# A two-block transformer on one core: block order of the down projection, one expert tile between top-k and gates, and where the first early expert group is made

## What is computed

```python
def first_block(...):
    h = h + hybrid_mixer(rmsnorm(h), ...)
    h = h + cross_attention(rmsnorm(h), rmsnorm(mem), ...)
    h = h + conv_ffn(rmsnorm(h), w_up, ffn_dw_w, w_down)
    return rmsnorm(h, norm_final_g)

def conv_ffn(h, w_up, ffn_dw_w, w_down):
    up = causal_dwconv(einsum("bsd,df->bsf", h, w_up), ffn_dw_w)
    z = silu(up[..., :D_FF]) * up[..., D_FF:]          # D_FF = 2816 = 22 blocks of 128
    return einsum("bsf,fd->bsd", z, w_down)

def second_block(...):
    ...                                                 # stick-breaking attention, gated delta rule, merge
    x = x + peer_ffn(rms_norm(x), w_q, keys1, keys2, u_tab, v_tab)

def peer_ffn(h, ...):                                   # 8 heads, 128 x 128 = 16384 experts, 16 per head
    s1, s2 = scores of the two halves of the query against 128 keys each
    v1, i1 = top_k(s1, 16); v2, i2 = top_k(s2, 16)
    vals, c = top_k(all sums v1 + v2, 16)
    expert, gate = from (i1, i2, c), softmax(vals)
    act = gelu(h @ u_tab[expert])                       # one column of u per chosen expert
    return sum over chosen experts of gate * act * v_tab[expert]
```

## Time and profile before

| what | us |
|---|---|
| median of 3 runs | 3472.61 (3469.71 to 3473.6) |
| the profiled execution's own time | 3472.78 |
| its span (first to last instruction) | 3470.6 |
| TensorE busy in it | 3325.0 (96%) |
| VectorE busy | 2271.6 (65%) |
| GpSimd busy | 1835.0 (53%) |
| ScalarE busy | 773.9 (22%) |
| DMA, mean over the span | 113 GB/s |

### The profile page before, as it was taken

One profiled execution on the slowest core, in us unless ns is written; L12 is line 12 of the kernel. 1 busy time (PEld: TensorE's weight loads), 2 busy tenths in 40 slices (PEclk: granted clock), 3 DMA queues, 4 the chain that ended last, 5 costly groups with the idle time before them and its releaser, 6 DMA issues.

```text
span 3470.6 us, 40765 instructions
## 1 busy us (share of the span) xinstructions
PE 3325.0 (96%) x15978; PEld 2735.4 (79%) x15978; DVE 2271.6 (65%) x3397; ACT 773.9 (22%) x1201; POOL 1835.0 (53%) x994
## 2 busy tenths in 40 slices
PE   7989899999999999899999999999999999999998
PEld 5777678877876787888788888888888887888887
DVE  7975279953316255776563888799964334787784
ACT  2132322211126222222211111145531111111110
POOL 4536267766442454100466666633346665676675
PEclk9999999999999999999999999999999999999999
DMA  3212122222220121000232344345553335555552
GB/s 134 73 55 97 43 90 96 96 89 89 99 71 33 61 86 66 20 13 13 85 106 98 140 138 142 137 158 204 188 203 119 118 122 182 194 191 191 190 186 98
DMA packets 164270, 391.70 MB, mean 113 GB/s; under 512 B 10736, under 2 KB 69104, under 8 KB 162032
## 3 DMA queue, kind: packets, MB, share of 16 engines
q1 hardware_dynamic: 73408, 262.70, 22.2%
q10 hardware_dynamic: 90672, 126.39, 10.7%
HBM read 326.14 MB, written 62.91 MB: 112 GB/s over the span
## 4 chain that ended last, share of the span: by engine, by line
PE 71%; DVE 24%; issue 2%; ACT 2%; POOL 0%; DMA 0%; ACTq 0%; DVEq 0%; POOLq 0%
PE banks L1381 19%; PE banks L1382 19%; PE banks L1383 19%; DVE sb_gated L1287 6%; DVE sb_sq L2026 3%; DVE sb_onehot L1284 2%; PE banks L704 1%; PE banks L367 1%; PE banks L715 1%; DVE sb_tmp L2036 1%; PE banks L712 1%; DVE banks L1903 1%; PE banks L384 1%; DVE sb_tmp L1327 1%; DVE sb_cacc L1903 1%
## 5 line engine op out<-in xcount | busy, mean ns | idle before, releaser
L1369 POOL TENSOR_TENSOR sb_wL<-sb_raw,sb_wH 128x1024 fp32r<-128x1024 f32 x495 | 1209.1, 2443 | 1604.1 <-PE banks L1383 1538.5
L1381 PE MATMUL banks<-sb_hH,sb_wH 128*128 128x512 f32 x2040 | 820.2, 402 | 9.1 <-DVE sb_hL L496 2.6
L1382 PE MATMUL banks<-sb_hL,sb_wH 128*128 128x512 f32 x2040 | 798.9, 392 | 0.0
L1383 PE MATMUL banks<-sb_hH,sb_wL 128*128 128x512 f32 x2040 | 798.8, 392 | 0.0
L1364 POOL TENSOR_SCALAR sb_wH<-sb_raw 128x1024 fp32r<-128x1024 f32 x495 | 641.9, 1297 | 14.6 <-DMA sb_raw<-in_weights 14.6
L1381 PEld LDWEIGHTS banks<-sb_hH,sb_wH 128*128 128x128 f32 x2040 | 386.4, 189 | 95.8 <-issue 14.8
L1383 PEld LDWEIGHTS banks<-sb_hH,sb_wL 128*128 128x128 f32 x2040 | 385.5, 189 | 82.2
L1382 PEld LDWEIGHTS banks<-sb_hL,sb_wH 128*128 128x128 f32 x2040 | 386.3, 189 | 77.9 <-issue 3.6
L1381 PE MATMUL banks<-sb_pzH,sb_wH 128*128 128x512 f32 x1024 | 401.7, 392 | 13.5 <-DVE sb_pzL L1331 11.3
L1382 PE MATMUL banks<-sb_pzL,sb_wH 128*128 128x512 f32 x1024 | 399.6, 390 | 0.0
L1383 PE MATMUL banks<-sb_pzH,sb_wL 128*128 128x512 f32 x1024 | 399.5, 390 | 0.0
(11 more groups left out here) (420 smaller groups left out, 4804.5 us busy)
## 6 DMA issues: line engine op xcount, KB each, us to landing
sb_raw<-in_weights SPq DMA_DIRECT2D x495, 512.0 KB, 3.2
gates<-sb_stage ACTq DMA_DIRECT2D x16, 2048.0 KB, 7.8
acts<-sb_sq ACTq DMA_DIRECT2D x96, 256.0 KB, 2.0
sb_Gt<-gates ACTq DMA_DIRECT2D x24, 1024.0 KB, 7.0
sb_Ga<-acts ACTq DMA_DIRECT2D x24, 1024.0 KB, 10.4
sb_Gt<-gates ACTq DMA_DIRECT2D x4, 2048.0 KB, 10.1
sb_xT<-in_xT SPq DMA_DIRECT2D x4, 512.0 KB, 10.2
acts<-sb_xT ACTq DMA_DIRECT2D x1, 2048.0 KB, 7.8
```

What stands on the lines that cost most here:

```text
L1369: nc.gpsimd.tensor_tensor(wL[:, t % LOS, :], raw[:, t % RAWS, :], wH[:, t % HIS, :].bitcast(F32), ALU.subtract).then_inc(sems("weights_lo" ...
L1381: pe.matmul(out, hi, H, start=start, stop=False)
L1382: pe.matmul(out, hi, L, start=False, stop=False)
L1383: return pe.matmul(out, lo, H, start=False, stop=stop)
```

## The change

1. A list `DOWN` gives the order of the 176 blocks of the down projection: rows d = 0 and d = 1 share it, first f = 0 to 15 of row 0, then f = 0 to 15 of row 1, then f = 16 to 21 of row 0 and of row 1. The other rows are as they were. The host packs the weights in the same order.
2. Between top-k and gates the meeting goes. TensorE runs one early u tile behind the last `turn_slots` and ACT its gelu; DVE waits only for the 12 copies to `sb_slots`. As the early u tiles are 96 as before, 31 of them are left for the 32 gate steps, and the last step has its four products without a tile.
3. In the last late group DVE no longer adds the 8 v tiles in a loop of its own. `early_group(-1, 0)` adds them one by one between the parts of early group 0.

```diff
+DOWN = [(_d, _f) for _f0, _f1 in ((0, 16), (16, FFB)) for _d in (0, 1) for _f in range(_f0, _f1)]
+DOWN += [(_d, _f) for _d in range(2, KB) for _f in range(FFB)]
...
             turn_slots(3)
-            E.meet()
+            one_tile(t0 + n, h_hi, h_lo)
+            n += 1
...
                 gate_products(4 * i + 1)
-                one_tile(t0 + n, h_hi, h_lo, ready=lambda k: gate_products(4 * i + k // 3 + 1) if k in (3, 6) else None)
+                if n < 8 * EARLY:
+                    one_tile(t0 + n, h_hi, h_lo, ready=lambda k: gate_products(4 * i + k // 3 + 1) if k in (3, 6) else None)
+                else:
+                    gate_products(4 * i + 2)
+                    gate_products(4 * i + 3)
...
             keep_slots(3)
-            E.meet()
+            early_gelu(n)
+            n += 1
...
-                    if r % 4 == 3:
+                    if r % 4 == 3 and n < 8 * EARLY:
                         early_gelu(n)
...
-            E.meet()
+            E.eng.wait_ge(sems("slots_copied"), 12)
             for j in range(TG):
...
-                for d in range(8):
+                for d in range(8 if g < LATE - 1 else 0):
                     t = t0 + 8 + d
                     tile_ready(E, t)
...
-                    if i is not None and e < 8:
+                    if e < 8:
                         t = t0 + 8 * i + e
                         tile_ready(E, t)
...
-                early_group(z - 1 if z else None, z if z < EARLY else None)
+                early_group(z - 1, z if z < EARLY else None)
...
-                        d, f = divmod(8 * (t - t0) + k, FFB)
+                        d, f = DOWN[8 * (t - t0) + k]
...
-    downs = down.reshape(FFB, P, 8, P).transpose(2, 0, 1, 3).reshape(22, 8, P, P).transpose(0, 2, 1, 3).reshape(22, P, D)
+    blocks = down.reshape(FFB, P, 8, P).transpose(2, 0, 1, 3)
+    downs = np.stack([blocks[d, f] for d, f in DOWN]).reshape(22, 8, P, P).transpose(0, 2, 1, 3).reshape(22, P, D)
```

## The result

The kernel after takes **3453.84 us** (median of 4 runs, 3452.01 to 3455.37), the kernel before 3472.61 beside it (4 runs, 3469.71 to 3473.6). The ratio is 0.9947 [0.9935, 0.9959]: 0.5% faster, 18.8 us. 3455.3 was predicted. The span of the profiled execution fell from 3470.6 to 3453.0, by 17.6.

The account below looks back on a forecast made before the run. TensorE was taken to set 71% of the time, with VectorE setting the gates' pace. Terms of 8.0 + 0.9 + 8.5 = 17.4 us off 3472.78 gave 3455.4, on the median 3455.2; it said 3455.3, range 3450 to 3462.

Parts of the forecast that it names:

- the time of the last z: Down projection: VectorE makes the last z at 737.65, or 740.7 with one GpSimd low part costing 3.02 us.
- rival 3: Down projection: two GpSimd parts cost 6.0 us, z comes 1.3 us late, up to 4; 3457 to 3459, chance 0.07.
- margin of 1.7 us: Down projection: the last z, at 740.7, still comes 1.7 us ahead of its block at 742.4.
- The early start: Start of the gates: TensorE's early start is used up by waiting, so the start of the rows hardly moves.
- (c): Gates: VectorE is behind from the start, so its 1.1 us of idle time go: -1.1 us.
- (a): End of the gates: the last step has no tile, only a product of about 0.9 us: -3.3 us.
- The second path: Last gates store to first late group's load to fifth late tile: store goes out at about 2569.4, 0.9 us earlier.
- The bound of +1: Tile between top-k and gates: +1 us if the 1.1 us do not come back and the store-load chain not either.
- rival 2: Early group 0: its load lands 3 us later, TensorE stops at tile 3; 3458 to 3461 us, chance 0.09.
- pays in full: Tile between the stages: GpSimd's extra part hides and both paths move by 3.9 us; 3452.3 us, chance 0.12.
- another rhythm: Gates: VectorE finds its ring full in every step, then is locked out by GpSimd; 34 us, 3489 in all, chance 0.02.
- missing large term: One of the two large terms is missing, for instance through another stop right behind; 3463.5 us, chance 0.05.

Follow-up runs that it names:

- e10: The kernel after with the first two down rows split at f = 19 instead of 16: 3452.77 us in one run.
- e9: The kernel after with the first two down rows split at f = 12 instead of 16: 3461.47 us in one run.
- e11: The kernel after with the two halves of early group 0 loaded in the other order, second half first: 3466.62 us in one run.
- second comparison: The kernel after, unchanged, measured once more against the kernel before: 3459.0 us against 3470.27, ratio 0.9958.
- e2: The kernel before with the tile between top-k and gates alone: 3473.92 us, ratio 1.001.
- e1: The kernel before with the new order of the down blocks alone: 3465.53 us, ratio 0.9983.
- e3: The kernel before with early group 0 made beside the last late v tiles alone: 3463.09 us, ratio 0.9979.

## Why the prediction came out as it did

The total is right: 3453.84 lies in 3450 to 3462, 1.5 us from 3455.3. Its working is right in two terms and wrong in one.

**Part 1 held** (-8.0 predicted, -7.6 measured). That the low clock would go with the wait held too: of the 7.6 us only 5.30 were idle. The Trainium skill (TensorE: Matmul & The Clock Gate, section "What's actually happening") has the halved clock as the idle state; by that rule more than the idle time is saved, and the runs agree (7.6 against 5.3). The step that was too generous is the time of the last z. One low part of GpSimd was reckoned on its way, there were two (behind tiles 2 and 3, at 736.82 and 742.26), as rival 3 had it. The prediction's own numbers had the second: tile 3 ends one tile, 5.44 us, behind tile 2's 733.5, so ahead of its z at 740.7. Against the start of the loop z came 25.5 us behind it, which is 742.7 in the times of before, not 740.7; the block was due at 742.4. Rival 3's mechanism was there, its price 0.4 us instead of 1.3 to 4, since the second part met only the two last low parts of z (3.48 us instead of 1.47) and TensorE went on without a longer stop. The margin of 1.7 us was in truth none; a split at 19 gives it, as e10 shows.

**Part 2 failed** (-0.9 predicted, +2.5 measured). Two steps of it held. The early start was used up by waiting: the first row comes only 0.1 us earlier. And GpSimd's work behind the extra tile costs 3.0 (306.0 - 302.9 = 3.1; the earlier trace rows gave 3.02). The Trainium skill (SBUF - State Buffer, section "SBUF: two separate sides") says that the loser of the shared port waits for a whole instruction of the other. The prediction set that against the low part's 2.43 us alone; with the high part behind it GpSimd works for 3.5 us, and the measured 3.0 to 3.1 stays below that, so the rows don't speak against the page.

Two steps failed. First (c), that VectorE's 1.1 us of idle time go because it is behind from the start: it stood idle for 1.2 us all the same. The extra part held back its second row, TensorE waited 2.82 us for that row and then ran at the low clock, and VectorE found its ring full at rows 7 and 8; in e9, with the clock at 1.00 there, the idle time is gone. Second (a), -3.3 us for the empty last step, with its product "at full clock": from the last gated to the first late tile it took 2.39 us instead of 0.9, so 1.8 were saved and not 3.3, and the late tiles behind it, the first at the low clock, lost 1.4 that the prediction put at nothing. The pieces are -0.1, +3.1, -1.8 and +1.4, together the +2.5 of the stretch within 0.1. Both failed steps are one: the prediction had priced the low clock wherever a stop went, and forgot it where one was made. The second path did not count: the store went out at 2559.82, the load at 2566.27, and the fifth late tile did not wait. (The prediction's 2569.4 for that store is 0.2 above its own terms, 2567.2 + 0.9 + 1.1; it changes nothing here.)

```profile
2559.82 0.33 ACTq L1004 DMA_DIRECT2D gates<-sb_stage  x1
2566.27 0.38 ACTq L1015 DMA_DIRECT2D sb_Gt<-gates  x1
```

The bound of +1 that stood for this term was too narrow by 1.5, since it left out the stop.

**Part 3 held** to the tenth: 6.27 us over the border as the row for groups 0 and 1 said, and 5.80 us of waiting for `sb_Ga`. The margin at the bank was 1.8 us (2883.3 against 2885.1); e11 shows what would have been lost: its half comes 8.9 us later and costs 9.1, where rival 2 had 3 to 5.5 for a half 3 us late.

**The rest was luck.** 4.0 us of the 17.6 between the two profiles come from stretches that the change doesn't touch. With 3459.0, the median of the second comparison, the forecast would have been 3.7 us too low, and still within its range. The rivals "pays in full" (part 2 -3.9) and "another rhythm" (+34) are out by e2: +2.4 in the stretch. That a missing large term would show is answered by e1 and e3, in which each large term is whole.

## What to carry to other kernels

Price a stop that a change makes as you price one that it takes away: idle time plus the matmuls behind it at the low clock. Here the meeting's removal brought nothing, since VectorE set the pace, the extra tile put 3 us more on VectorE, and the empty last step, which should have paid for that, saved 0.4 us instead of 3.3. Where one engine sets the pace of a stage and another of the next, put the other's work into the first up to where both meet: 8 tiles moved so gave 11 us, where the whole change gave 13.6. And when a change is worth 0.5%, cut both traces at marks that both have, since here untouched code differed by more than one of the three terms.

## What was not expected of the hardware

- While GpSimd makes a low part and the high part behind it, 3.5 us together, VectorE's gated beside them take 3.0 us longer, nearly the whole of that time (4.13 us for four instead of 1.11). With the low part cut to 0.55 us it is 0.9 for each tile, and VectorE's rows fell by 19.6 us.
- The granted clock fell from 1.00 to 0.50 in a step in which TensorE did 16 short matmuls, stood idle for 2.19 us and did 16 more. Behind a wait of 2.82 us it was at 0.50 in five profiles and at 1.00 in one of the same code (e9).
- The same instructions over 1465 us took between 1463.0 and 1473.6 us in fourteen profiles, with granted clocks of 0.97 and 1.00 at the same place.
